# A hybrid decoder step on one Trainium2 core: expert blocks of 32 slots in four column groups

## The reference

```python
logits = (xt @ w_router) + b_router
topv, topi = top_k(logits, 4)            # 4 of 32 experts a token
wts = softmax(topv)
...
gu = xb @ w_gu[e] + b_gu[e]              # (slots, 1024) @ (1024, 2048)
gate = minimum(gu[:, :1024], 7.0)
up = clip(gu[:, 1024:], -7.0, 7.0)
act = (up + 1.0) * gate * sigmoid(1.702 * gate)
y = (act @ w_down[e] + b_down[e]) * w    # (slots, 1024) @ (1024, 1024)
```

## Time and profile before

| | |
|---|---|
| Median of 3 runs | 1699.89 us (1699.86 to 1700.97) |
| Profiled execution, its span | 1698.1 us |
| TensorE busy | 1574.4 us, 93% |
| VectorE, ScalarE, GpSimd busy | 526.8, 270.9, 61.0 us |
| DMA | 505.57 MB, mean 298 GB/s over the span |
| First bias product of the experts | 613.70 us |
| Last sum of the experts ends | 1674.67 us |

### The profile page before, as it was taken

One profiled execution on the slowest core, in us unless ns is written; L12 is line 12 of the kernel. 1 busy time (PEld: TensorE's weight loads), 2 busy tenths in 40 slices (PEclk: granted clock), 3 DMA queues, 4 the chain that ended last, 5 costly groups with the idle time before them and its releaser, 6 DMA issues.

```text
span 1698.1 us, 21861 instructions
## 1 busy us (share of the span) xinstructions
PE 1574.4 (93%) x7876; PEld 703.7 (41%) x7877; DVE 526.8 (31%) x1142; ACT 270.9 (16%) x527; POOL 61.0 (4%) x113
## 2 busy tenths in 40 slices
PE   5798989989999699999999999999999999999995
PEld 2335665557766443333333333333333333333332
DVE  2325554616444412222131312212222122222223
ACT  2014441221110221111010010100111101010101
POOL 2002220000010000000000000000000000000000
PEclk8899999978899889999999999999999999999997
DMA  9525896560065239879999999999999979996920
GB/s 334 204 72 199 301 382 251 184 221 1 0 224 216 99 149 409 332 295 410 410 409 410 410 409 409 410 409 409 410 410 409 410 298 400 409 410 250 398 104 31
DMA packets 146156, 505.57 MB, mean 298 GB/s; under 512 B 6559, under 2 KB 6679, under 8 KB 145890
## 3 DMA queue, kind: packets, MB, share of 16 engines
q1 hardware_dynamic: 138178, 480.08, 72.6%
q0 software_dynamic: 7936, 24.94, 4.5%
HBM read 499.88 MB, written 5.11 MB: 297 GB/s over the span
## 4 chain that ended last, share of the span: by engine, by line
PE 67%; SPq 16%; DMA 7%; DVE 6%; ACT 2%; issue 2%; DVEq 0%; POOL 0%; ACTq 0%; POOLq 0%
PE psum L506 62%; SPq L2209 16%; DMA ring<-in_w_gu 6%; PE psum L665 2%; ACT region L1775 1%; PE psum L959 1%; DMA ring<-in_w_ada 1%; DVE region L1277 1%; PE psum L1031 1%; PE psum L697 0%; DVE hT L1163 0%; DVE region L1244 0%; DMA region<-in_c_sample 0%; DVE region L1560 0%; DVE region L1766 0%
## 5 line engine op out<-in xcount | busy, mean ns | idle before, releaser
L506 PE MATMUL psum<-ring,region 128*64 128x512 f32 (+1 forms) x3968 | 792.9, 557 | 24.0 <-DMA ring<-in_w_gu 23.1
L506 PEld LDWEIGHTS psum<-ring,region 128*64 128x64 f32 (+1 forms) x3968 | 253.5, 134 | 482.8 <-issue 423.1
L1775 ACT ACTIVATE region<-psum 128x512 f32<-128x512 f32 (+7 forms) x296 | 154.1, 538 | 885.1 <-PE psum L506 775.7
L506 PE MATMUL psum<-region 64*128 64x320 f32 (+9 forms) x1446 | 270.2, 491 | 4.9 <-ACT region L1775 3.5
L1685 DVE TENSOR_SCALAR region<-psum 128x512 f32<-128x512 f32 x36 | 24.9, 691 | 645.1 <-PE psum L506 645.1
L506 PEld LDWEIGHTS psum<-region 64*128 64x128 f32 (+5 forms) x1446 | 112.1, 159 | 175.2 <-issue 158.1
L1677 DVE TENSOR_TENSOR region<-region,psum 128x640 f32<-128x640 f32 x144 | 111.7, 817 | 114.1 <-PE psum L506 114.1
L506 PE MATMUL psum<-hT,ring 128*128 128x320 f32 x448 | 124.6, 436 | 0.0
L506 PEld LDWEIGHTS psum<-hT,ring 128*128 128x128 f32 x448 | 84.7, 192 | 35.4 <-issue 1.9
L506 PE MATMUL psum<-ring,hT 128*128 128x512 f32 (+1 forms) x192 | 86.7, 608 | 6.1 <-DVE hT L1169 6.1
L2048 ACT ACTIVATE region<-region 128x512 f32<-128x512 f32 x36 | 22.7, 630 | 293.4 <-DVE region L1685 293.4
(11 more groups left out here) (300 smaller groups left out, 858.7 us busy)
## 6 DMA issues: line engine op xcount, KB each, us to landing
ring<-in_w_gu SPq DMA_DIRECT2D x128, 2048.0 KB, 21.7
ring<-in_w_down SPq DMA_DIRECT2D x64, 2048.0 KB, 18.8
ring<-in_w_ada SPq DMA_DIRECT2D x12, 2048.0 KB, 14.4
ring<-in_w_in SPq DMA_DIRECT2D x11, 2048.0 KB, 19.6
ring<-in_cache_k SPq DMA_DIRECT2D x64, 256.0 KB, 5.4
ring<-in_cache_v POOLq DMA_DIRECT2D x64, 256.0 KB, 5.5
ring<-in_w_out SPq DMA_DIRECT2D x2, 2048.0 KB, 20.4
ring<-in_w_up_a SPq DMA_DIRECT2D x1, 2048.0 KB, 10.2
```

Of the source, the lines that this page charges most:

```text
L506: return pe.matmul(out, lhsT, rhs, start=start, stop=stop, skip_group_check=True)
L1775: return act.activation(out, src, ACT.Copy)
```

## The change

- A block has 32 slots instead of 64 (SLOTS), so an expert has one block for each 32 tokens begun. The stationary operand takes 32 columns of the array, and four products run side by side (`spread`): PSUM rows 32c to 32c + 31 hold output columns 256c to 256c + 255. The tiles behind (`act_g`, `hg_rows`, `y_rows`, ...) are 256 columns wide instead of 512.
- Gate and up are done together, one quarter of the contraction (256 rows of `w_gu`, all 2,048 columns) to a unit; down is two units of 512 rows.
- In memory a partition takes two neighbouring rows (2p and 2p + 1), so one run is 16 KB for `w_gu` and 8 KB for `w_down`. The transposes of the gathered rows and of the activation take every second column to match.
- A block's down stands in the next block, behind that one's second quarter; `combine` is two calls of four products (four row groups of 32) instead of four calls of two, and both sums are 1,280 wide.
- The slot tables and their constants grow (10 rounds for 5); those constants are loaded by POOL ahead of the router's weights instead of at the start.

The diff, cut to what orders the work on TensorE, VectorE, ScalarE, SP and POOL; waits in it are those of the new kernel:

```diff
-SLOTS = 64
+SLOTS = 32
+GROUPS = P // SLOTS
+WIDE = FF // GROUPS
...
-            def pair(out_bank, lhsT, rhs_at, start, stop):
-                for h, rows in enumerate((H0, H1)):
-                    last = mm(psum[rows, out_bank, :], lhsT, rhs_at(h), start, stop)
+            def spread(out_bank, lhsT, rhs_at, start, stop):
+                for c in range(GROUPS):
+                    last = mm(psum[LANES[c], out_bank, 0:WIDE], lhsT, rhs_at(slice(WIDE * c, WIDE * c + WIDE)),
+                              start, stop)
                 return last
...
             def turn_gathered():
-                for i in range(4):
-                    last = pe.transpose(psum[:, B_HG_T, P * i:P * i + P], hg_rows[:, P * i:P * i + P], ident)
+                rows = hg_rows.rearrange("q (p j) -> q j p", j=2)
+                for j in range(2):
+                    last = pe.transpose(psum[:, B_HG, P * j:P * j + P], rows[:, j, :], ident)
...
+            def gate_up_quarter(c, expert):
+                pe.wait_ge(unit_landed[moe_slot[c]], 16 * expert + (landed_base[c] + 16))
+                u = ring[:, moe_slot[c], :].rearrange("p (j f) -> p j f", j=2)
+                for j in range(2):
+                    for q, out_bank in ((0, B_GATE), (1, B_UP)):
+                        last = spread(out_bank, hgT[:, j, LANES[c]],
+                                      lambda cols: u[:, j, FF * q + cols.start:FF * q + cols.stop],
+                                      False, c == 3 and j == 1)
+                last.then_inc(unit_read[c], 1)
...
+            def combine(r):
+                for c in range(GROUPS):
+                    last = mm(psum[:, B_SUM + c, 0:NT], y_rows[LANES[c], P * r:P * r + P],
+                              selwT[LANES[c], :], True, True)
+                last.then_inc(combined, 1)
...
+            def expert_block(b, expert, before_expert, first):
+                pe.wait_ge(hgT_copied, b + 1)
+                pe.wait_ge(bias_hot_ready, b + 1)
+                if not first:
+                    pe.wait_ge(gate_clamped, b)
+                    pe.wait_ge(up_clamped, b)
+                bias_rows()
+                gate_up_quarter(0, expert)
+                if not first:
+                    pe.wait_ge(act_ready, b)
+                    pe.wait_ge(selwT_copied, b)
+                    turn_act()
+                gate_up_quarter(1, expert)
+                if not first:
+                    pe.wait_ge(actT_copied, b)
+                    down(before_expert)
+                pe.wait_ge(sel_ready, b + 2)
+                gather(b + 1)
+                gate_up_quarter(2, expert)
+                if not first:
+                    pe.wait_ge(y_copied, b)
+                    combine(0)
+                gate_up_quarter(3, expert)
+                pe.wait_ge(hg_copied, b + 2)
+                turn_gathered()
+                if not first:
+                    pe.wait_ge(added, 2 * b - 1)
+                    combine(1)
+                pe.wait_ge(selw_ready, b + 1)
+                turn_weights()
...
             def expert_block(b, column, expert, next_column, next_expert, first):
...
+                dve.tensor_scalar(act_g, psum[:, B_GATE, 0:WIDE], LIMIT, None, ALU.min).then_inc(gate_clamped, 1)
+                dve.tensor_scalar(act_u, psum[:, B_UP, 0:WIDE], LIMIT, -LIMIT, ALU.min, ALU.max)\
                     .then_inc(up_clamped, 1)
+                hot(next_expert)
...
                 if not first:
-                    dve.wait_ge(added, 4 * b)
+                    add_sums(b - 1, 1)
...
             for part in range(3):
                 pool.dma_start(bias_f32[NE * part:NE * part + NE, :], I["b_gu"]).then_inc(bias_in, 16)
+            pool.dma_start(late_const, I["const"][:, n_late:n_const]).then_inc(moe_in, 16)
             pool.dma_start(w_rt, I["w_router"].rearrange("(k p) e -> p k e", p=P)).then_inc(moe_in, 16)
...
-            gu = I["w_gu"].rearrange("e (k p) f -> e p k f", p=P)
-            dn = I["w_down"].rearrange("e (k p) f -> e p k f", p=P)
+            gu = I["w_gu"].rearrange("e (c p j) f -> e c p (j f)", c=4, j=2)
+            dn = I["w_down"].rearrange("e (h c p j) f -> e h p c (j f)", h=2, c=2, j=2)
```

More of the change, by code:

```diff
@@ L119, in const_pack, with build @@
     put("drop", np.tile(np.where(start, BIG, 0).astype(np.float32), (H, 1)))
-    return np.concatenate(cols, 1), at, keep
-def build(nc, I, O, const_at, n_const, n_keep):
+    late = n
+    put("before", (i[:, None] < i[None, :]).astype(np.float32))
+    put("slots", np.tile(i % SLOTS, (P, 1)).astype(np.float32))
+    put("round_start", np.tile(np.repeat(-1.0 - SLOTS * np.arange(ROUNDS), NE), (P, 1)).astype(np.float32))
+    put("rounds", np.tile(np.arange(1, ROUNDS) * SLOTS + 0.5, (P, 1)).astype(np.float32))
+    return np.concatenate(cols, 1), at, keep, late
+def build(nc, I, O, const_at, n_const, n_keep, n_late):
     ctx = ExitStack()
@@ L248, in build @@
         bias_f32 = Area(E.at + KT * NT).take(2 * FF)
[L249 to L255, removed]
+        act_g = E.take(WIDE)
+        act_s = E.take(WIDE)
+        act_u = E.take(WIDE)
+        hg_rows = E.take(WIDE)
+        y_rows = E.take(WIDE)
+        actT = E.take(2, P)
+        hgT = E.take(2, P)
+        fin_junk = E.take(512)
+        fin_add = E.take(512)
         sel = E.take(3, SLOTS)
@@ L263, in build @@
         eq = E.take(3, NE)
-        pos = E.take(3, ROUNDS * NE)
         part_logits = E.take(NT)
@@ L284, in build @@
         assert E.at <= REGION - KT * NT
+        pos = E.take(3, ROUNDS * NE)
         y_out = h2_tok
@@ L960, in turn_gathered @@
+                for j in range(2):
+                    last = pe.transpose(psum[:, B_HG, P * j:P * j + P], rows[:, j, :], ident)
                 last.then_inc(hg_turned, 1)
[L962 to L1025, removed]
-                last.then_inc(act_turned, 1)
[L1027 to L1036, removed]
@@ L1037, in expert_block, with turn_act, down @@
+            def turn_act():
+                rows = act_u.rearrange("q (p j) -> q j p", j=2)
+                for j in range(2):
+                    last = pe.transpose(psum[:, B_Y, P * j:P * j + P], rows[:, j, :], ident)
+                last.then_inc(act_turned, 1)
+            def down(expert):
                 for half in range(2):
@@ new lines, in down @@
+                    for c in range(2):
+                        for j in range(2):
+                            last = spread(B_Y, actT[:, j, LANES[2 * half + c]], lambda cols: u[:, c, j, cols],
+                                          half == 0 and c == 0 and j == 0, half == 1 and c == 1 and j == 1)
+                    last.then_inc(unit_read[i], 1)
+            def combine(r):
[3 more added lines that the diff above has]
+                last.then_inc(combined, 1)
@@ L1730, in _ @@
                              bass.ds(next_expert, 1), False)
-            blocks = later + 1
-            for i in range(4):
-                add_sums(blocks, i)
-            dve.wait_ge(added, 4 * blocks)
+            for r in range(2):
+                add_sums(later, r)
+            dve.wait_ge(added, 2 * later + 2)
             steps[0], steps[1] = 0, tail_step
@@ L2068, in _ @@
             later = act.value_load(ints[0:1, AT_LATER:AT_LATER + 1], min_val=NE - 1, max_val=MAX_BLOCKS - 1)
-            with act.Fori(0, later) as p:
+            copy_act_and_rows(0, True)
+            expert_block(1, False)
+            with act.Fori(1, later) as p:
+                copy_act_and_rows(p, False)
                 expert_block(p + 1, False)
+            copy_act_and_rows(later, False)
             act.wait_ge(fin_ss_set, 1)
-            act.wait_ge(hgT_copied, later + 2)
             for half in range(2):
```

160 lines of the change are left out of this document (80 added, 80 removed).

## The result

The changed kernel takes 1676.44 us (median of 4 runs, 1661.14 to 1680.99) beside 1700.43 us before: a ratio of 0.9855, 95% interval 0.9821 to 0.9889. A second measurement, of 6 runs, gave 1679.73 beside 1699.61, ratio 0.9892 (0.9861 to 0.9923). So it is faster, by 20 to 24 us (1.1 to 1.5%); the forecast was 1,644, 56 us faster. Sign and range held, and less than half of the gain came. The profiled execution took 1677.65 us with a span of 1675.4, 33 us over the 1642 of the forecast's sum.

What follows compares the result with a forecast made beforehand. The expert stage was taken as bound by TensorE, with DMA just under it. From 1698.1, the stage's 59.1 came off and 3 for the clock went on: 1642, with the span 1.8 under the median, so 1,644 us; range 1,626 to 1,695.

Steps and rivals of the forecast that it cites:

- T: TensorE's time for one block of 32 slots: terms sum to 15.2 us, taken as 15.3, bounds 14.8 and 17.7.
- Fours and further changes of shape: Gate, up and down in a block: 48 fours at 0.22 us make 10.6; further changes of shape 0.4.
- Transposes (rows, activation, weights): TensorE's transposes in a block: four take 0.5 us, the three of the weights 0.5.
- Two combines: Two combine calls a block, 0.7 us each if the four row groups run nearly together: 1.4 us.
- Two-block experts behind two-block ones: An expert following a two-block one starts late and takes 2T = 30.6 us; seven times 1.1 make 8 us.
- Three-block experts: Second block's down waits for the last unit, leaving DMA idle 13.9 us; three times (3, 24, 29) make 42.
- the clock's term: Loss to TensorE's clock: from 0 to some 4 us in each of seven one-to-two-block passages (28); taken as 3 us.
- Rival (a): Weight rows are cut into 4 KB packets, so DMA stays at 30.7 us an expert: 1,673 us, chance 0.16.
- Slower (0.13): Whole kernel slower than before, by a rival whose description is cut from the text or another cause: chance 0.13.
- Rival (c): T near 16.7 us, half-way to its upper bound: about 1,690 us, chance 0.09.
- 2.4 a block would be exposed: Activation's five operations take 2.4 us, hidden by 3.5 us of TensorE work; without that cover, 2.4 a block shows.
- in time by 1.7 us: At a two-block expert, the next expert's first unit flows by 27.8 us after the start, ahead of 29.5.

Runs made afterwards that it cites:

- edge run: One of TensorE's two register loads at the loop's edge moved behind the first quarter, against the changed kernel: 1660.71 us, ratio 0.9759 to the kernel before.
- trim: On the edge run's kernel, combine's second call straight behind the fourth quarter and the wait for turned rows behind the bias: 1654.93 us, again 1656.88.
- warm: On the edge run's kernel, 16 unused matmuls fill the wait for the next expert's first unit behind one-block experts, with two more register loads: 1674.62 us.
- warm_trim: On the edge run's kernel, the edits of warm and trim together: 1672.49 us, ratio 0.9863 to the kernel before.

## Why the prediction was right in sign and wrong in size

**The step that failed is the sum for T**, "15.2; I take 15.3". It is 15.93. What was mis-sized in it can be read off the block above, from the start of each group to the start of the next:

| Term of the sum | forecast, us | measured, us |
|---|---|---|
| Fours and further changes of shape | 10.6 + 0.4 | 1.85 + 5.20 + 1.87 + 1.87 = 10.79 |
| Gather | 1.5 | 1.54 |
| Two combines | 1.4 | 0.75 + 0.76 = 1.51 |
| Transposes (rows, activation, weights) | 0.5 + 0.5 | 0.43 + 0.43 + 0.65 = 1.51 |
| Bias | 0.3 | 0.22 |
| Idle at the loop's edge | none | 0.38 |
| Sum | 15.2 | 15.95 |

The unknown prices, of a four of 256 columns and of a combine, were about right. Wrong were the plain ones, the transposes by 0.5 us and the loop's edge by 0.4. I had priced transposes at the mean inside a row of four, though they now come as two groups of two, each with its own change of shape. And I hadn't looked at what stands at the loop's edge: the old block has one register load there, behind a down product of 7.09 us; the new one has two, behind three short transposes. The edge run moved one of the two, and the idle time went.

How much of the 33 us is this? When T was brought to 15.33 (trim), to what the forecast had, the time was 1655 to 1657: some 21 us are T. The other 12 are the steps around it. The forecast let expert 31 flow at 1550.8 and 3 later for the clock, 1553.8. In the trace it is 1553.50 + 1.5 + 29.5 (the expert before it has one block) = 1584.5, 31 late. By place (D is DMA's time for an expert, 29.5 us):

- Two-block experts behind two-block ones: seven rows of SP's queue, 31.81 to 32.19, in sum 17.1 over D, forecast 8. Nearly all of it is T: 2T - D is 2.4, not 1.1, and seven times that is 16.5.
- Three-block experts: 47.77 - 29.5 = 18.3, and with the one-block expert next to them 17.6 and 18.7, forecast 13.9 each, 12.9 more in all. Three times T's 0.63 would be 1.9 of each. For expert 3 the step's premise fell too: behind two-block experts TensorE has no slack, and the idle is 3T - D. At the other two the first quarter had a granted clock of 0.59 and 0.50 (3.21 and 3.64 us), at expert 29 the second with down 0.75 (7.11).
- Passages from one block to two, the first expert's with them: 10.5 over D, forecast 3 as the clock's term. A passage of 35.20 costs nothing, one of 38.04 about 2 (with the expert before it 61.2, twice 29.5 is 59). Without the first expert they are 8.8, and in the second trace 12.0. With a shorter block, and the clock as it was, they were 0.3 (T = 15.48, edge) and 3.8 and 3.6 (T = 15.33, trim); with the waits filled too, between -1.3 and 0.2. So most of it goes with the block; what the clock adds is a few us at most, and how much stays open. The 3 us of the clock's term were an estimate that no run shows; what they show is a first quarter of 3.21 to 3.64 us instead of 1.93, at 0.59 to 0.50 of the clock.
- The start was 1.5 later, 615.84 instead of 614.3, and the end some 3 longer.

**What was right.** There are 55 blocks: the bias group counts 440 records, 8 a block. Rows of 16 and 8 KB go as long packets (33,036 of 8 KB and more) and give 424 to 428 GB/s where DMA is saturated, forecast 429 and 422: 29.5 us an expert. Inside a block nothing is late, the activation's chain included. TensorE's matmuls with the expert weights wait 120 us for DMA, where the forecast had some 150. Rival (a) falls by the packets. Slower (0.13) didn't come, and the queue of code has 27 packets in all against 25, one of them after 667 us, so none for each round; the gap at this loop's jump was 0.37 us (17.5 us over 47 times) and went with a register load. Rival (c), a longer T, was the direction in which it went, half as far.

**What was right by luck.** Moving down was priced by what it hides, "2.4 a block would be exposed". The 102 to 105 us of the run without it, 1.9 a block, look like that number, but they are the ring's: the block was only 0.6 longer, and TensorE waited for down's units. My timing of the units with down moved (in time by 1.7 us) was about right: the passages come out between 0.6 us in time and some 3 late, with T 0.63 longer in each block. Had I done the same arithmetic for down in its place, it would have shown which part the smaller blocks can't do without.

## What to carry to other kernels

With a ring that holds one stage of work, ask for each unit when it is wanted and when its slot comes free; moving the consumer of the last units half a round later can be worth more than any cheaper instruction (here 102 to 105 us), and smaller blocks without it can lose (here 7%). When a block shrinks, price each group's change of shape and the loop's edge anew: here one change of shape less, with one wait placed later, took a block from 15.48 to 15.33 us, a second register load behind short transposes cost 0.38 us a block, and two more in the middle of the block 0.28. Where one engine is barely ahead of DMA, a gain in a block counts only at the places where TensorE sets the pace, so count those places first (here some 35 us for each us of a block, with 55 blocks).

## What the hardware showed that I had not expected

- Behind a wait of 7.5 to 10.8 us the first quarter had a granted clock of 0.50 to 0.59 in every passage of the changed kernel. What the piece behind it did, after a further wait of 0.6 to 1.25 us, changed from trace to trace: it took 6.96 to 7.59 us at 0.77 to 0.70, instead of 5.39 at 1.00, in 3 to 8 of 12 passages in the six traces without a fill. With the first of the two waits filled it was slow (6.86 to 7.07 us, at 0.78 to 0.76) in 10 and in 4 of 12 (warm and warm_trim). Only with both filled (28 matmuls) did it have 1.00 in all 12, and that bought no time that these runs could tell.
- Kernels that hardly differ ahead of the experts reach the first bias product between 605.12 and 614.73 us, so single profiled runs of theirs can't be compared by their spans. The changed kernel's own times go from 1661 to 1684 us; what makes them differ by so much isn't shown.
